# First feed-forward: seven quarter products for the second half's hidden groups, and the modulation sums laid out anew

## The chip, the cores and the metric

The kernel runs on one core of one Trainium2 chip, as one program. The metric is the device time of one execution in microseconds (us). The kernel before takes 2897.2 us, the median of three runs (2896.49 to 2897.56).

## What is computed

The reference runs 512 tokens of width 1024 through two stacks of layers. The change touches the first of them, whose layers are modulated by a condition vector `c`:

```
cond = jax.nn.silu(c)
mod = (cond @ ada_w[i] + ada_b[i]).reshape(b_, N_SUBLAYERS, 3, D_MODEL)
h = adaln(x, norm_g[i, 0], mod[:, 0, 0], mod[:, 0, 1])
x = x + 0.5 * (1.0 + mod[:, 0, 2][:, None, :]) * swiglu(h, ffn_w_in[i, 0], ffn_w_out[i, 0])
...
def swiglu(h, w_in, w_out):
    g, u = jnp.split(h @ w_in, 2, axis=-1)
    return (jax.nn.silu(g) * u) @ w_out
```

All products are in float32 accuracy. There are six modulated sublayers, numbered s = 0 to 5; 0, 2, 3 and 5 are feed-forwards of this kind with 2816 hidden columns, 1 is a pooling mixer and 4 an attention. `cond @ ada_w` asks for 6 x 24 = 144 sums of 128 outputs each. Sixteen of them (shift and scale of s = 0) are needed before the first layer can begin, the other 128 are "modulation sums" in what follows, in the order s = 0 (8 of them, the gate), then 24 for each later s.

## The kernel before, in words

Weights come from HBM as chunks of 128 x 1024 floats (512 KB) into a ring of four buffers, `raw`. Each chunk is split into a high part `wh` (ScalarE, L697) and a low part `wl` (VectorE, L1263, the "weight split"), and TensorE makes three products for each 128 x 128 block of weights: high by high, high by low, low by high. The activations are split alike: `HH` and `HL` are the normed input of a feed-forward, `AH` and `AL` the hidden activations. A ring buffer may be split again when TensorE has used its chunk, so a split is at most four chunks ahead.

A feed-forward is done in two halves. Each half has a first map (6 or 5 hidden groups of 256 hidden columns, each with four chunks: 8 input tiles, 4 output tiles, so 96 matmuls of 512 columns) and a second map (12 or 10 chunks, in two banks of four output tiles). A hidden group ends with silu on ScalarE, a product and the low part on VectorE (`hidden_group`, L1603 and L1622). The two halves of `PS` (PSUM) are used in turn: a group may begin when the group two before it has been read (`bank_free`).

In the feed-forwards s = 2, 3 and 5 most hidden groups are "fast groups" (4 of 6 and 5 of 5; the table `FAST`): the matrix product is cut in four quarters of weights and four quadrants of activations, and made by seven quarter products, not eight. A fast group has 7 x 24 = 168 matmuls of 256 columns (L2478 to L2480). It wants four mixed quadrants of the input, made once per feed-forward by VectorE and ScalarE (`whole`, `mixed_input`, `mix_low`, `mix_high`: 12 VectorE instructions), and for each group four sums of weight quarters and seven splits on VectorE (`fast_low`: L1654 is the split, L1657, L1660, L1662 and L1664 the sums). The products of a fast group follow each other as (i, 1), (i, 7), (i, 6), (i, 2), (i, 5), (i, 3), (i, 4), with (i+1, 1) ahead of (i, 3). Six buffers hold the quarters: the four of `raw` and two halves of `WK`. SyncE issues these loads in order at L581, and the first two go into `WK`.

The modulation sums are VectorE instructions over 128 x 1024 (`ada_sum`, L1333; the sum is read out by a short second instruction). Their weights, 512 KB each, are loaded by GpSimd's queue: the first 80 into a ring of three tiles (L618), all during s = 0; then 24 each in s = 2 and s = 3 (L626) into four tiles: `piece`, `HT` and the two halves of `WK`. `ADA_PHASES` says that 16 of these lie in the first half's second map and 8 in the second half's. `splits_with_sums` puts a number of sums behind each weight split.

At the start of the fast groups of a second half, VectorE makes `fast_low` for two products, adds the second map's result to `X` (`add_out`, L1328) and goes on with `fast_low` for the third:

```
for k in range(early):
    fast_low(part, k)
if between:
    between()
...
for k in range(early, RING):
    fast_low(part, k)
```

Of the kernel before, what the change touches and what calls it, by code (L numbers as in the profile page):

```python
# [20 lines left out]
ALU = mybir.AluOpType  # L21
# [38 lines left out]
ADA_RING = 3  # L60
# [71 lines left out]
def make_plan(upto=None):  # L132
# [24 lines left out]
    for i, (kind, f) in enumerate(seq):  # L157
# [12 lines left out]
        elif kind == "ffn":  # L170
            st["parts"], st["sets"] = [], sum(bool(p.get("parts")) for p in plan[:-1])
            for half, (ng, nt) in enumerate(f["halves"]):
                nf = (f.get("fast") or (0, 0))[half]
                if nf:
# [5 lines left out]
                                            tile=2 * (ng - nf), sums=ADA_BY[f["gate"]] - ADA_PHASES[1] if late else 0))  # L180
# [35 lines left out]
def build(nc, A, out, upto=None):  # L216
    plan, NCH = make_plan(upto)
    ctx = ExitStack()
    with ctx:
# [27 lines left out]
        with ExitStack() as temps:  # L247
# [36 lines left out]
        ada_late = [piece[:, 0:1024], HT[:, :, :].rearrange("p a t -> p (a t)"),  # L284
                    *(WK[:, 2 * i:2 * i + 2, :].rearrange("p k t -> p (k t)") for i in range(2))]
        ada_tiles = [acc[:, 1, 1024:2048], acc[:, 1, 2048:3072], piece[:, 0:1024]]
# [46 lines left out]
        def mix_raw(i):  # L333

            o = 2048 + 1024 * i + (2048 if i >= 4 else 0)
            return arena[:, o:o + 1024].rearrange("p (k t) -> p k t", k=4)
# [61 lines left out]
        ada_in = [sem(f"ada_in{i}") for i in range(ADA_RING)]  # L398
        ada_late_in = [sem(f"ada_late_in{i}") for i in range(4)]
# [112 lines left out]
        def _(sp):  # L512
# [34 lines left out]
            sp.dma_start(bands[:, 0:NBAND], A["params"][:, NCOL:NCOL + NBAND]).then_inc(bands_in, 16)  # L547
# [36 lines left out]
            for st in plan:  # L584
                for part in st.get("parts", ()):
# [6 lines left out]
                    loaded = part["c"] + RING  # L592
            load_chunks(loaded, NCH)
# [10 lines left out]
        def _(pl):  # L604
# [9 lines left out]
            pl.wait_ge(ada0_step, 14)  # L614
            for m, (s, j) in enumerate(ADA_ORDER[:ADA_EARLY]):
                if m >= ADA_RING:
                    pl.wait_ge(ada_step, m + 1 - ADA_RING)
                pl.dma_start(ada_tiles[m % ADA_RING], A["stream"][NCH + s * NADA + j, :, :]).then_inc(ada_in[m % ADA_RING], 16)  # L618
            m = ADA_EARLY
            for st in plan:  # L620
                for part, n in zip(st.get("parts", ()) if st.get("gate") in ADA_BY else (), ADA_PHASES):
                    pl.wait_ge(a_ready, part["e"] + part["n"] + 1)
                    for i in range(n):
                        pl.wait_ge(ada_step, max(m - 3, ADA_EARLY))
                        s, j = ADA_ORDER[m]
                        pl.dma_start(ada_late[m % 4], A["stream"][NCH + s * NADA + j, :, :]).then_inc(ada_late_in[m % 4], 16)  # L626
                        m += 1
# [57 lines left out]
        def _(act):  # L685
# [202 lines left out]
            def mix_high(i, sets):  # L888

                act.wait_ge(mix_sum, 4 * sets + i + 1)  # L890
                src = mix_raw(4 + i)
# [51 lines left out]
            for st in plan:  # L943
# [32 lines left out]
                elif kind == "ffn":  # L976
                    e, cv, j = st["e"], st["cv"], 0
                    c_last = c + sum(4 * ng + nt for ng, nt in st["halves"]) - 4 * sum(part["n"] for part in st["parts"])
                    for ng, nt in st["halves"]:
                        pairs = ng // 2  # L980
                        if st["parts"]:
                            part = st["parts"][c > st["c"]]
                            if c == st["c"]:
                                if part is fast_parts[0]:
                                    F(condc, condb, ACT.Copy).then_inc(cond_moved, 1)
                                    act.wait_ge(cond_moved, 1)
# [11 lines left out]
                        if st is plan[2] and c == st["c"]:  # L998
# [22 lines left out]
                        if st is plan[2] and c < c_last - nt:  # L1021
                            late_constants()
                        for half in range(2):
                            if half == 1 and c + nt // 2 == c_last:
                                tilewise_tail(st, c, nt)
                            else:
                                split_until(c + nt // 2 + RING)
                            c += nt // 2
# [220 lines left out]
        def _(dve):  # L1249
# [46 lines left out]
            def late_constants():  # L1296
# [5 lines left out]
                link(nc.vector.tensor_tensor_reduce(WK[:, 0, 0:64], P("lam", 0, 64), P("lam", 64, 64), 1.0, 0.0,  # L1302
                                                    ALU.mult, ALU.add, lam[:, 0:1]))
                nc.vector.tensor_tensor_reduce(WK[:, 0, 64:128], P("lam", 128, 64), P("lam", 192, 64), 1.0, 0.0,
                                               ALU.mult, ALU.add, lam[:, 1:2]).then_inc(lam_dot, 1)

                for i, (nm, f) in enumerate([("fq", 0.125), ("fk", 1.0), ("aq", 0.125), ("ak", 1.0), ("bq", 0.125),
                                             ("bk", 1.0), ("bsub", (1.0 - 0.2) * math.sqrt(128))]):
                    TS(gains[:, i:i + 1], P(nm), f, None, ALU.mult)
                dve.wait_ge(sp_exp, 1)  # L1310
# [20 lines left out]
            def ada_sum(tile, s, j, cond=condb):  # L1331

                return nc.vector.tensor_tensor_reduce(tile, tile, cond, 1.0, 0.0, ALU.mult, ALU.add, mod[:, s, j:j + 1])  # L1333
# [38 lines left out]
            def ada_until(n):  # L1372

                while at["ada"] < n:
                    m = at["ada"]
                    s, j = ADA_ORDER[m]
                    if m < ADA_EARLY:
                        dve.wait_ge(ada_in[m % ADA_RING], 16 * (m // ADA_RING + 1))
                        ada_sum(ada_tiles[m % ADA_RING], s, j).then_inc(ada_step, 1)
                    else:  # L1380
                        dve.wait_ge(ada_late_in[m % 4], 16 * ((m - ADA_EARLY) // 4 + 1))
                        ada_sum(ada_late[m % 4], s, j, condc).then_inc(ada_step, 1)
# [241 lines left out]
            def whole(k, t, i):  # L1624

                link(TT(mix_raw(i), quadrant(HH, k, t).bitcast(F32), quadrant(HL, k, t).bitcast(F32), ALU.add))

            def mixed_input(i, a, b, op):

                dve.wait_ge(vec_step, at["step"])  # L1630
                if op is None:
# [1268 lines left out]
```

## Time and profile before

| | |
|---|---|
| median of three runs | 2897.2 us |
| time of the profiled execution | 2896.0 us |
| its span, first to last instruction | 2893.6 us |
| TensorE matmuls busy | 2873.8 us (99%) |
| VectorE busy | 1939.4 us (67%) |
| ScalarE busy | 1264.7 us (44%) |
| TensorE's mean granted clock | 0.999 |

The time of an execution is 2.4 us longer than its span. Busy time of TensorE is a union of overlapping instructions, so at 99% the question is at what pace the matmuls follow each other, and where they don't.

### The profile page before, as it was taken

The page shows a single profiled execution, that of the slowest core. Times are in us where ns is not written, and L with a number is a line of the kernel's source. Part 1 is how long each engine was busy: PE and PEld are TensorE (multiplying, and loading weights), DVE is VectorE, ACT ScalarE, POOL GpSimd, SP SyncE. Part 2 cuts the span into 40 slices and gives each one's busy share as a digit, 9 for nine tenths or more (in the row PEclk, how much of TensorE's full clock was granted, in tenths as well). Part 3 has the DMA queues.
Part 4 walks back from the last instruction along what each step waited for, and adds up shares of the span by engine and source line. Part 5 has one row for each costly group of instructions (what it writes and reads, how often), then busy time and mean ns, then how long its engine had stood idle before and what let it go on. Part 6 is the DMA issues. An engine that isn't in the chain of part 4 may idle for free. (4 is left out here: it accounts for less than half of the span.)

```text
span 2893.6 us, 40922 instructions
## 1 busy us (share of the span) xinstructions
PE 2873.8 (99%) x16099; PEld 2485.7 (86%) x16099; DVE 1939.4 (67%) x2624; ACT 1264.7 (44%) x1752; POOL 144.9 (5%) x297
## 2 busy tenths in 40 slices
PE   8999999999999999999999999999999999999999
PEld 7888889899898998868999988788888888888887
DVE  8667688777786777876856758766535467754453
ACT  4223255344452445474533445654414348443332
POOL 0111100100001001040000000200000001000000
PEclk9999999999999999999999999999999999999999
DMA  7867613524236243251332322413232222232231
GB/s 299 272 217 255 210 45 115 206 109 154 89 115 230 91 168 107 88 182 61 108 126 79 114 91 88 160 63 110 87 105 98 95 81 95 96 108 95 88 109 66
DMA packets 100944, 366.99 MB, mean 127 GB/s; under 512 B 11248, under 2 KB 11808, under 8 KB 100784
## 3 DMA queue, kind: packets, MB, share of 16 engines
q1 hardware_dynamic: 77616, 276.56, 27.9%
q0 software_dynamic: 23168, 88.17, 8.8%
q8 instruction: 116, 1.90, 0.3%
q14 instruction: 44, 0.36, 0.0%
HBM read 362.51 MB, written 2.18 MB: 126 GB/s over the span
## 5 line engine op out<-in xcount | busy, mean ns | idle before, releaser
L1263 DVE TENSOR_TENSOR wl<-raw,wh 128x1024 fp32r<-128x1024 f32 x393 | 477.1, 1226 | 519.4 <-ACT wh L697 518.9
L697 ACT ACTIVATE wh<-raw 128x1024 fp32r<-128x1024 f32 x393 | 409.8, 1054 | 752.4 <-PE PS L2131 685.1
L2131 PE MATMUL PS<-HH,wh 128*128 128x512 f32 x1560 | 608.2, 390 | 0.4 <-DVE HL L1979 0.3
L2131 PE MATMUL PS<-HL,wh 128*128 128x512 f32 x1560 | 607.7, 390 | 0.0
L2131 PE MATMUL PS<-HH,wl 128*128 128x512 f32 x1560 | 607.7, 390 | 0.0
L2131 PEld LDWEIGHTS PS<-HH,wh 128*128 128x128 f32 x1560 | 293.1, 188 | 62.1 <-DVE HL L1979 0.8
L2131 PEld LDWEIGHTS PS<-HH,wl 128*128 128x128 f32 x1560 | 293.0, 188 | 60.5
L2131 PEld LDWEIGHTS PS<-HL,wh 128*128 128x128 f32 x1560 | 293.1, 188 | 60.3
L2131 PE MATMUL PS<-AH,wh 128*128 128x512 f32 x848 | 330.7, 390 | 0.5 <-DVEq L2014 0.5
L2131 PE MATMUL PS<-AL,wh 128*128 128x512 f32 x848 | 330.5, 390 | 0.0
L2131 PE MATMUL PS<-AH,wl 128*128 128x512 f32 x848 | 330.3, 390 | 0.0
L2480 PE MATMUL PS<-HH,wl 128*128 128x256 f32 x864 | 245.0, 284 | 0.0
L2479 PE MATMUL PS<-HL,wh 128*128 128x256 f32 x864 | 245.0, 284 | 0.0
L2478 PE MATMUL PS<-HH,wh 128*128 128x256 f32 x864 | 244.9, 283 | 0.0
L2131 PEld LDWEIGHTS PS<-AH,wh 128*128 128x128 f32 x848 | 159.3, 188 | 33.7 <-DVEq L2014 0.9
L2131 PEld LDWEIGHTS PS<-AH,wl 128*128 128x128 f32 x848 | 159.3, 188 | 33.0
L2131 PEld LDWEIGHTS PS<-AL,wh 128*128 128x128 f32 x848 | 159.4, 188 | 32.5
L2480 PE MATMUL PS<-TH,wl 128*128 128x256 f32 x648 | 183.8, 284 | 0.0
L2478 PE MATMUL PS<-TH,wh 128*128 128x256 f32 x648 | 183.7, 284 | 0.0
L2479 PE MATMUL PS<-TL,wh 128*128 128x256 f32 x648 | 183.7, 284 | 0.0
L1654 DVE TENSOR_TENSOR wl<-raw,wh 128x1024 fp32r<-128x1024 f32 x117 | 142.7, 1222 | 38.6 <-ACT wh L910 38.6
L2479 PEld LDWEIGHTS PS<-HL,wh 128*128 128x128 f32 x864 | 166.1, 192 | 0.5
(346 smaller groups left out, 5107.6 us busy)
## 6 DMA issues: line engine op xcount, KB each, us to landing
raw<-in_stream SPq DMA_DIRECT2D x459, 512.0 KB, 3.4
acc<-in_stream POOLq DMA_DIRECT2D x54, 512.0 KB, 4.9
WK<-in_stream SPq DMA_DIRECT2D x42, 512.0 KB, 4.5
piece<-in_stream POOLq DMA_DIRECT2D x38, 512.0 KB, 5.0
WK<-in_stream POOLq DMA_DIRECT2D x24, 512.0 KB, 6.6
arena<-in_stream SPq DMA_DIRECT2D x16, 512.0 KB, 12.5
HT<-in_stream POOLq DMA_DIRECT2D x12, 512.0 KB, 6.8
TBa<-negcum POOLq DMA_DIRECT2D x8, 640.0 KB, 5.0
```

Source lines behind the costliest of these rows:

```text
L697: F(wh[:, r, :], raw[:, r, :], ACT.Copy).then_inc(hi_done, 1)
L1263: TT(wl[:, r, :], raw[:, r, :], wh[:, r, :].bitcast(F32), ALU.subtract).then_inc(lo_done, 1)
L1654: TT(wl[:, r, :], src, wh[:, r, :].bitcast(F32), ALU.subtract).then_inc(fast_lo, 1)
L2131: mm = MM(PS[g % 2][:, j, :], l, x, start=(first and i == 0), stop=(last and i == 2), skip_group_check=after_halves)
L2478: MM(o, wh[:, r, w], xh, start=first, stop=False, skip_group_check=True)
L2479: MM(o, wh[:, r, w], xl, start=False, stop=False, skip_group_check=True)
L2480: mm = MM(o, wl[:, r, w], xh, start=False, stop=kk == 3, skip_group_check=True)
```

## The change

`FAST` gets the entry `0: (0, 5)`: the five hidden groups of the second half of the first feed-forward become fast groups. Their mixed input is made during the first half's plain groups. The modulation sums are laid out anew: 36 in the first half's plain groups of s = 0 (two behind each split, three in the last group), then 20 and 10 in its second maps; 20 and 11 in those of s = 2 and of s = 3. All of them use one list of seven tiles (`ADA_PLACES`), the last four of a first half only `piece` and `HT`. The spread condition vector lies in `bands` (`condc`) from the start, so the bands of the pooling mixer are loaded late and the vector is moved away and back. The small constants for later layers (`late_constants`) move into the first half's second map and are cut in two, with `late_factors` behind `add_out`.

```diff
-FAST = {2: (4, 5), 3: (4, 5), 5: (4, 5)}
-ADA_BY = {0: 8 + 3 * NADA, 2: 8 + 4 * NADA, 3: 8 + 5 * NADA}
-ADA_EARLY = ADA_BY[0]
-ADA_PHASES = (16, 8)
+FAST = {0: (0, 5), 2: (4, 5), 3: (4, 5), 5: (4, 5)}
+ADA_EARLY = 36
+ADA_PHASES = {0: (20, 10), 2: (20, 11), 3: (20, 11)}
+ADA_BY = {0: 66, 2: 97, 3: 128}
+ADA_PLACE = [2, 3, 0] + [4, 5, 6]
+def late_places():
+
+    places = []
+    for into_part, behind in ADA_PHASES.values():
+        places += [(0, 1, 2, 3)[i % 4] if i < into_part - 4 else i % 2 for i in range(into_part)]
+        places += [(0, 1, 2, 3)[i % 4] for i in range(behind)]
+    return places
...
-                                            tile=2 * (ng - nf), sums=ADA_BY[f["gate"]] - ADA_PHASES[1] if late else 0))
+                                            tile=2 * (ng - nf), sums=max(m + 1 for m in range(ADA_BY[f["gate"]] - ADA_PHASES[f["gate"]][1])
+                                                      if ADA_PLACES[m] in (2, 3)) if late else 0))
...
-            pl.wait_ge(ada0_step, 14)
-            for m, (s, j) in enumerate(ADA_ORDER[:ADA_EARLY]):
-                if m >= ADA_RING:
-                    pl.wait_ge(ada_step, m + 1 - ADA_RING)
-                pl.dma_start(ada_tiles[m % ADA_RING], A["stream"][NCH + s * NADA + j, :, :]).then_inc(ada_in[m % ADA_RING], 16)
+            pl.wait_ge(ht_done, KT)
+            def load_ada(m):
+
+                if ada_free(m):
+                    pl.wait_ge(ada_step, ada_free(m))
+                (s, j), place = ADA_ORDER[m], ADA_PLACES[m]
+                pl.dma_start(ada_tiles[place], A["stream"][NCH + s * NADA + j, :, :]).then_inc(ada_in[place], 16)
...
+                    if part:
+                        pl.wait_ge(a_ready, part["e"] + part["n"] + 1)
                     for i in range(n):
+                        if not part and ADA_PLACES[m] == 1:
+                            pl.wait_ge(mix_ready, 4)
+                        load_ada(m)
                         m += 1
...
+                            act.wait_ge(ada_step, ADA_EARLY)
+                            for i in range(4):
+                                mix_high(i, st["sets"])
...
+                                    ada_until(at["ada"] + (3 if u == 5 else 2))
+                                    if (u, i) == (2, 1):
+                                        whole(0, 0, 0, sets)
+                                    elif (u, i) == (2, 3):
+                                        whole(0, 1, 1, sets)
+                                    elif (u, i) == (3, 0):
+                                        mixed_input(0, sets)
...
+                            for i in range(4):
+                                mix_low(i, sets)
...
-                                splits_with_sums(c + nt // 2 + RING, 2 if st["parts"] else 1, ada or at["ada"])
-                                if half == 1 and st["parts"]:
-                                    fast_groups(st, st["parts"][1],
+                                ahead = c + nt != c_last and st["at"][1]
+                                most = 0 if ada is None else ada - ADA_PHASES[st["gate"]][1] if ahead else ada
+                                if st is plan[2] and half == 0 and ahead:
+                                    late_constants()
+                                splits_with_sums(c + nt // 2 + RING, 2, most)
+                                if half == 1 or not ahead:
+                                    ada_until(most)
+                                if half == 1 and ahead:
+                                    fast_groups(st, ahead,
                                                 lambda: add_out(st, g, c + nt // 2, 4, gate))
                                 else:
                                     add_out(st, g, c + nt // 2, 4 * half, gate)
+                                if st is plan[2] and half == 0 and ahead:
+                                    late_factors()
```

VectorE in s = 0, where the first half's second map ends and the second half's first map begins (`piece` and `acc` are the tiles of weights for sums, `X` the residual). Before:

```order
L1263 TENSOR_TENSOR wl<-raw,wh 128x1024
L1333 ISA piece,mod<-piece,acc 128x1024
L1333 ISA mod 128x1
L1263 TENSOR_TENSOR wl<-raw,wh 128x1024
L1333 ISA acc,mod<-acc 128x1024
L1333 ISA mod 128x1
L1263 TENSOR_TENSOR wl<-raw,wh 128x1024
L1333 ISA acc,mod<-acc 128x1024
L1333 ISA mod 128x1
L1328 SCALAR_TENSOR_TENSOR X<-PS,mod,X 128x512 x4
```

The same place in the changed kernel, from the second sum in `WK` behind the last split (L1701 and L1704 are `fast_low`'s split and first sum of quarters):

```order
L1381 ISA WK,mod<-WK,bands 128x1024
L1381 ISA mod 128x1
L1381 ISA piece,mod<-piece,bands 128x1024
L1381 ISA mod 128x1
L1381 ISA HT,mod<-HT,bands 128x1024
L1381 ISA mod 128x1
L1381 ISA piece,mod<-piece,bands 128x1024
L1381 ISA mod 128x1
L1381 ISA HT,mod<-HT,bands 128x1024
L1381 ISA mod 128x1
L1546 TENSOR_TENSOR mod<-mod,par 128x24
L1548 SCALAR_TENSOR_TENSOR mod<-mod,par 128x8
```

One more instruction on `mod` follows and then L1701. Four sums with no split between them now stand ahead of the first quarter split, where each sum stood behind a split before.

VectorE at the end of the first half's last plain group in s = 0 (L1603 and L1622 are `hidden_group`). Before:

```order
L1263 TENSOR_TENSOR wl<-raw,wh 128x1024
L1333 ISA acc,mod<-acc 128x1024
L1333 ISA mod 128x1
L1603 TENSOR_TENSOR PR<-SG,PS 128x1024
L1622 TENSOR_TENSOR AL<-PR,AH 128x1024
```

And in the changed kernel, where L1647 and L1666 are `hidden_group`, and L1688 and L1690 the low parts of the mixed input:

```order
L1308 TENSOR_TENSOR wl<-raw,wh 128x1024
L1381 ISA acc,mod<-acc,bands 128x1024
L1381 ISA mod 128x1
L1381 ISA acc,mod<-acc,bands 128x1024
L1381 ISA mod 128x1
L1381 ISA acc,mod<-acc,bands 128x1024
L1381 ISA mod 128x1
L1647 TENSOR_TENSOR PR<-SG,PS 128x1024
L1666 TENSOR_TENSOR AL<-PR,AH 128x1024
L1688 TENSOR_TENSOR TL<-acc,TH 128x1024 x3
L1690 TENSOR_TENSOR HL<-HT,HH 128x4x256
```

Two more sums stand behind the last split, and four low parts behind the group.

## Rows read from the trace of the kernel before

**Rows 1.** The page: busy time, share of the span, instructions

```profile
PE 2873.8 (99%) x16099; PEld 2485.7 (86%) x16099; DVE 1939.4 (67%) x2624; ACT 1264.7 (44%) x1752; POOL 144.9 (5%) x297
```

**Rows 2.** Waits of TensorE: line, who released it; us in total, times, longest

```profile
PE PS L2492 <- DMA ident<-in_ident: 3.3, 1, 3.3
PE PS L2247 <- ACT HH L761: 2.2, 1, 2.2
...
PE PS L2131 <- DVE HL L1979: 0.3, 1, 0.3
```

**Rows 3.** Timeline of TensorE, s = 0: start us, us; second maps and plain groups begin

```profile
149.06 0.39 PE L2131 MATMUL PS<-AH,wh 128*128 128x512 f32 x1
...
214.34 0.39 PE L2131 MATMUL PS<-HH,wh 128*128 128x512 f32 x1
...
323.14 0.39 PE L2131 MATMUL PS<-AH,wh 128*128 128x512 f32 x1
```

**Rows 4.** Timeline of TensorE, s = 2: its fast groups begin and end

```profile
454.76 0.28 PE L2478 MATMUL PS<-HH,wh 128*128 128x256 f32 x1
...
538.14 0.40 PE L2131 MATMUL PS<-AH,wh 128*128 128x512 f32 x1
...
600.72 0.28 PE L2478 MATMUL PS<-HH,wh 128*128 128x256 f32 x1
```

**Rows 5.** Windows, s = 0's last plain groups: us, busy of PE, PEld, DVE, ACT, POOL, clock, DMA, GB/s

```profile
128.00:150.00 22.00, 22.00 (x99) 18.23 (x98) 15.18 (x20) 6.34 (x7) 3.70 (x7) 1.00 0.79 260
```

**Rows 6.** Timeline of VectorE, s = 0: a last plain group's end, then the late constants

```profile
150.41 1.23 DVE L1263 TENSOR_TENSOR wl<-raw,wh 128x1024 fp32r<-128x1024 f32 x1 [1.92 <-ACT wh L697]
151.56 1.22 DVE L1333 CUSTOM_DVE_ANT_0 acc<-acc 128x1024 f32<-128x1024 f32 x1
152.70 1.22 DVE L1603 TENSOR_TENSOR PR<-SG,PS 128x1024 f32<-128x1024 f32 x1
155.04 1.23 DVE L1622 TENSOR_TENSOR AL<-PR,AH 128x1024 fp32r<-128x1024 f32 x1 [1.12 <-ACT AH L886]
...
157.33 0.17 DVE L1299 TENSOR_SCALAR sp<-par 128x8 f32<-128x8 f32 x1
...
158.66 0.16 DVE L1284 TENSOR_SCALAR sp<-sp 128x8 f32<-128x8 f32 x1
...
162.10 1.22 DVE L1263 TENSOR_TENSOR wl<-raw,wh 128x1024 fp32r<-128x1024 f32 x1
```

**Rows 7.** Timeline of VectorE, s = 2: from the sixteenth sum to the fast groups

```profile
582.60 1.22 DVE L1333 CUSTOM_DVE_ANT_0 WK<-WK,bands 128x1024 f32<-128x1024 f32 x1
583.75 0.08 DVE L1333 DVE_READ_ACCUMULATOR2_ANT mod<- 128x1 f32 x1
591.20 1.23 DVE L1654 TENSOR_TENSOR wl<-WK,wh 128x1024 fp32r<-128x1024 f32 x1 [7.37 <-ACT wh L910]
592.34 1.22 DVE L1657 TENSOR_TENSOR WK<-WK 128x1024 f32<-128x1024 f32 x1
596.63 1.23 DVE L1654 TENSOR_TENSOR wl<-WK,wh 128x1024 fp32r<-128x1024 f32 x1 [3.08 <-ACT wh L910]
597.78 1.22 DVE L1660 TENSOR_TENSOR WK<-WK,raw 128x1024 f32<-128x1024 f32 x1
599.03 1.22 DVE L1662 TENSOR_TENSOR WK<-WK 128x1024 f32<-128x1024 f32 x1
600.92 2.73 DVE L1328 SCALAR_TENSOR_TENSOR X<-PS,mod,X 128x512 f32<-128x512 f32 x4 [0.67 <-PE PS L2131]
603.57 1.22 DVE L1654 TENSOR_TENSOR wl<-WK,wh 128x1024 fp32r<-128x1024 f32 x1
```

**Rows 8.** Instructions on the tile HT, 530 to 610 us: its loads

```profile
DMA to landing us min/median/max: 3.8/6.0/7.6
```

**Rows 9.** Timeline of SyncE's queue, s = 2: the first six loads of quarters

```profile
583.91 0.81 SPq L581 DMA_DIRECT2D WK<-in_stream  x2
584.78 2.06 SPq L581 DMA_DIRECT2D raw<-in_stream  x4
```

**Rows 10.** DMA in 575 to 605 us: rate in 40 slices, then KB and us to landing

```profile
GB/s 306 300 169 38 5 0 0 0 11 0 0 0 0 153 306 415 431 410 410 421 426 426 421 355 22 0 0 0 0 0 0 0 0 0 0 0 22 0 0 0
...
raw<-in_stream SPq DMA_DIRECT2D x4, 512.0 KB, 6.6
```

**Rows 11.** Windows around the pooling mixer, columns as in group 5

```profile
400.00:404.00 4.00, 2.69 (x19) 2.12 (x17) 4.00 (x11) 2.30 (x5) 0.00 (x0) 1.00 0.09 37
404.00:408.00 4.00, 3.29 (x18) 3.26 (x18) 3.12 (x12) 1.41 (x4) 0.00 (x0) 0.67 0.00 0
408.00:412.00 4.00, 3.19 (x22) 2.92 (x22) 3.42 (x9) 2.28 (x6) 0.00 (x0) 0.90 0.00 0
```

More of the change, by code:

```diff
@@ L170, in make_plan @@
         elif kind == "ffn":
-            st["parts"], st["sets"] = [], sum(bool(p.get("parts")) for p in plan[:-1])
+            st["parts"], st["at"], st["sets"] = [], [None, None], sum(bool(p.get("parts")) for p in plan[:-1])
             for half, (ng, nt) in enumerate(f["halves"]):
@@ L592, in _ @@
                     loaded = part["c"] + RING
+                if st is plan[2]:
+                    load_chunks(loaded, part["c"] + st["halves"][1][1] + 1)
+                    loaded = part["c"] + st["halves"][1][1] + 1
+                    sp.wait_ge(cond_moved, 1)
+                    sp.dma_start(bands[:, 0:NBAND], A["params"][:, NCOL:NCOL + NBAND]).then_inc(bands_in, 16)
             load_chunks(loaded, NCH)
@@ L1775, in _ @@
                     ada = ADA_BY.get(st["gate"])
[L1776 to L1777 removed]
+                    sets = st["sets"]
+                    for part, (ng, nt) in zip(st["at"], st["halves"]):
+                        if part:
                             if c == st["c"]:
[L1779 removed]
+                                dve.wait_ge(cond_moved, 2)
                                 dve.wait_ge(h_ready, st["h"])
[L1781 to L1783 removed]
+                                whole(0, 0, 0, sets)
+                                whole(0, 1, 1, sets)
+                                mixed_input(0, sets)
@@ L1801, in _ @@
-                        if ada and not st["parts"]:
-                            paired = st is plan[2] and c == st["c"]
-                            if paired:
-                                split_until(c + 10)
-                                hidden_group(st, e, g, cv, j, 0, 0)
-                                split_until(c + 11)
-                                hidden_group(st, e + 1, g + 1, cv + 1, j + 1, 2, 0)
-                                split_until(c + 12)
-                                e, cv, g, c, j = e + 2, cv + 2, g + 2, c + 8, j + 2
-                            for u in range(2 if paired else 0, ng):
+                                fast_groups(st, part, None)
@@ new lines, in _ @@
+                            e, cv, g, c, j, ng = e + ng, cv + ng, g + ng, part["c"], j + ng, 0
+                        elif st is plan[2]:
+                            split_until(c + 10)
+                            hidden_group(st, e, g, cv, j, 0, 0)
+                            split_until(c + 11)
+                            hidden_group(st, e + 1, g + 1, cv + 1, j + 1, 2, 0)
+                            split_until(c + 12)
+                            e, cv, g, c, j = e + 2, cv + 2, g + 2, c + 8, j + 2
+                            for u in range(2, ng):
@@ L1828, in _ @@
                         e, cv, g, c, j = e + 2 * pairs, cv + 2 * pairs, g + 2 * pairs, c + 8 * pairs, j + 2 * pairs
-                        if ng % 2 and not ada and not st["parts"]:
+                        if ng % 2 and not part:
                             split_until(c + 4 + RING)
@@ L2520, in _ @@
                                 group(c, g, KT, h_tile, h_ready_at, nm=nm)
-                                if not st["parts"] or st["parts"][0]["c"] > c + 4:
+                                if not st["at"][0] or st["at"][0]["c"] > c + 4:
                                     group(c + 4, g + 1, KT, h_tile)
                             c, g, e2, pairs, nm = c + 8, g + 2, e2 + 2, pairs - 1, None
-                        if st["parts"]:
-                            part = st["parts"][half]
+                        part = st["at"][half]
+                        if part:
                             fast_groups(st, part)
@@ L2541, in _ @@
                                 group(c, g, nt, a_tile, (lambda k: [(a_ready, e + k // 2 + 2)]),
-                                      begun=1 if half == 0 and st["parts"] else 0)
+                                      begun=1 if half == 0 and part else 0)
                             c, g = c + nt // 2, g + 1
```

136 lines of the change are left out of this document (72 added, 64 removed).

## The prediction, as it was made before the changed kernel ran

> **What bounds the kernel now.** I read the page first: TensorE's matmuls cover 99% of the span, VectorE 67% [rows 1]. Then the waits of TensorE: apart from the start, where it waits for inputs, no line waits more than some 2 us in total, and no fast-group line stands in the list at all [rows 2]. So TensorE's instruction stream sets the time, and an edit is worth what it takes out of that stream, less the waits that it makes. The timeline gives the pace. In s = 0 the second half's five plain groups run from 214.34 to 323.14 us [rows 3]: 480 matmuls in 108.80 us, 0.2267 us each, 21.76 us a group. In s = 2 four fast groups, with one unit of 12 plain matmuls put among them, run from 454.76 to 538.14 us [rows 4]: 83.38 us, less 12 x 0.2267 = 2.72, leaves 80.66, so 20.16 us a group and 0.120 us a matmul, exactly even. There was no wait in them.
>
> **What the change takes out.** Five groups, each 21.76 - 20.16 = 1.60 us: **8.0 us**. The bytes are the same (20 quarters for 20 chunks), and the unit of 12 is only moved. [...]
>
> **What it adds to VectorE, first half of s = 0.** One VectorE instruction over 128 x 1024 behind another costs 1.14 us: the split starts at 150.41, the sum at 151.56, the product at 152.70 [rows 6]. A plain group of 21.76 us now holds 4 splits, 8 sums, 2 instructions of the group and 2 or 3 of the mixed input: 16 or 17 instructions, 18.2 to 19.4 us, and with the 1.12 us for ScalarE's copy [rows 6] 19.4 to 20.5. The last has 12 sums and none of the input: 18 instructions, 21.6 us. Before it was 15.18 us of 22 [rows 5]. That just fits. A split is four chunks (21.8 us) ahead, less some 2.6 for both engines' parts, so VectorE may be some 14 us late before TensorE misses one. I put this at nothing. The loads go from 7 + 4 to at most 8 + 4 of 512 KB per group, 289 GB/s by their bytes where 260 at 0.79 of the DMA engines is the row [rows 5] and 431 the highest rate seen [rows 10]: also nothing.
>
> **Where it is late: the second map of the first half.** It begins at 149.06 us [rows 3] in both kernels. The last split of the plain group starts at 150.4 as now [rows 6]. Behind it: three sums until 155.0, product, ScalarE's copy and low part until 158.5, four low parts of the mixed input until 162.8 (ScalarE's highs, some 1.05 each, keep pace), first part of the late constants 1.3 us (157.33 to 158.66 [rows 6]), a split and a sum: 166.5. The second sum reads `HT`, whose load GpSimd may issue only after the fourth low part, at 162.8; such a load took 3.8 to 7.6 us, median 6.0 [rows 8]. So about 168.5. From there VectorE has 15 sums and 7 splits (22 x 1.14 = 25.1 us), `add_out` 2.7 us [rows 7] and `late_factors`, 158.66 to 162.10, 3.4 us [rows 6]: 199.7, say 200. In s = 2 the same sixteenth sum ends at 583.75 us [rows 7], 16.97 us before its fast groups; here it is 214.34 - 200 = 14.3 us before. Where four tiles can't be refilled in time, up to 2 us later still.
>
> **The four sums that stand alone.** The thirteenth sum ends 4.6 us before the sixteenth, so the reloaded `piece` is there 1.5 us after it (6.0 median), and the seventeenth and eighteenth sum end at 203.6. The twentieth reads `HT` again: load 6.0 us, sum 1.2 us: 210.9. Then the chain that s = 2 shows [rows 7]: three small instructions on `mod` (0.6), split 1.1, sum 1.25, ScalarE 1.15, split 1.3, two sums 2.4, `add_out` 2.65, the third split 1.2: 11.7 us, ends **222.6**. TensorE wants that third product at 214.34 + 2 x 24 x 0.120 = **220.1**. The wait is **2.5 us**. Behind it one split more is ready each time TensorE asks, and the wait is not given back, since TensorE has no slack. Bounds: `HT` in 3.8 us and the eighteenth sum at 202.0 give 218.8, no wait; 7.6 us and everything 2 us later give 226.3, a wait of 6.2.
>
> During these loads SyncE issues six quarters from the sixteenth sum on: in s = 2 at 583.91 to 586.8 [rows 9], and the engines run full at 410 to 431 GB/s for 7 us, so that a quarter in `raw` lands after 6.6 us [rows 10]. No row has a load of GpSimd's beside them; this is why I don't go below the median. The Trainium skill ("DMA: Bandwidth & Descriptors", section "Queues, rings and completion order") says that each DMA engine takes turns between the queues that have work, packet by packet. By that the load would not stand behind all six; in order behind them it would land some 9 us after its issue, 3 us more wait.
>
> **In s = 2 and s = 3** the same four sums and three more in the second half come in. VectorE is idle for 7.37 us there [rows 7]. Seventeenth and eighteenth end at 586.0, the twentieth at 586.1 + 6.0 + 1.2 = 593.3, the third split at 593.3 + 11.1 = 604.4, wanted at 600.72 + 5.76 = 606.5: no wait; with 7.6 us 606.0, still none. I count 0.1 us each, bound 1. Their second halves have 27 us for 11 sums; add_out is then some 4 us later and its next user waits for nothing in the rows. Nothing. The bands of the pooling mixer are loaded some 40 us ahead of their use: nothing.
>
> **Sum.** 8.0 - 2.5 - 0.2 = 5.3 us. The profiled execution took 2896.0 us and would take 2890.7; the median of the runs is 1.2 us above it, so **2891.9 us**.
>
> **Rivals.** (1) *All is hidden.* For it: fast groups show no wait anywhere [rows 2], and the least landing gives 218.8. Against it: nothing in s = 2 has the late constants, `add_out` and the input's low parts in the same stretch. Gain 6.8 to 8.0 us, 2889.2 to 2890.4. (2) *Larger waits.* `HT` lands after the six quarters, or the clock falls. TensorE was busy for 2.69 of 4 us around 402 us, and the granted clock was then 0.67 and 0.90 for 4 us each [rows 11]: between its levels of 1.2 and 2.4 GHz that is about 3.4 us at the lower, 1.7 us lost. With a wait of 4.5 to 6.2 us and this, the gain is 0 to 3.5 us: 2893.7 to 2897.2. (3) *Slower.* VectorE becomes the bound in the plain groups: if mixed input and sums there cost 3.5 us a group more than the ledger (because loads from GpSimd's queue come late, say), it ends the fourth group 14 us late, misses splits from then on, and all of it stands again ahead of the fast groups, since VectorE never comes to rest between. At 5 us a group it is 20 us late; less the 14 us of lead, 6 us of waits in the plain groups and 6 more ahead of the fast ones against 8 gained: 2901. It decides from about 4 us a group. Against it: 6.8 us of 22 are idle now [rows 5]. (4) *A quarter product is no faster in this place*: the pace is TensorE's own; I see nothing for it.
>
> **How the numbers follow.** A measurement of this kernel can tell about 0.2%, 5.8 us, from no change. My forecast (wait 1.2 to 4.5 us, gain 3.5 to 6.8) 0.47; all hidden 0.25; larger waits 0.20; slower 0.08. The forecast straddles the 5.8 us: 0.18 of its 0.47 lie above. Faster 0.25 + 0.18 = 0.43; slower by over 5.8 us 0.05; within 0.52. The range, 2888.8 to 2895.6, takes in the hidden case and half of the larger waits.
>
> **What would show it.** The first of s = 0's fast groups begins at 214.3 and its five take 5 x 20.16 us plus the wait; TensorE's waits list a fast-group line released by VectorE's quarter split, about 2.5 us, once, near 220 us, and none in s = 2 and 3. `late_factors` stands behind `add_out` near 190 us, the sixteenth sum near 200, the twentieth near 211. The plain groups keep their 21.76 us. I am wrong if there is no such wait, if it sits at the first product or in s = 2, or if TensorE waits before 214 us.

## The result, and the profile after

The changed kernel takes 2902.6 us (median of 8 runs, 2900.5 to 2908.1), the kernel before beside it 2896.6. The ratio is 1.0022, 95% interval 1.0013 to 1.0031. A second measurement gave 2899.5 us (11 runs, 2897.6 to 2903.3) against 2896.5, 1.0011 (1.0002 to 1.0020). So the change costs some 3 to 6 us; forecast were 5.3 gained. The profiled execution took 2901.7 us, its span is 2899.8. Two executions further down, 3527.4 us with four tiles and 3131.6 us with the late factors moved, ran at a mean granted clock of 0.75 and 0.85 and are left out of the ratios (the median of 2897.0 us given for the latter kernel is 2896.6 without it).

The page of the changed kernel, as [rows 1] of before:

```profile
PE 2870.9 (99%) x16459; PEld 2499.7 (86%) x16459; DVE 1998.3 (69%) x2681; ACT 1288.6 (44%) x1784; POOL 145.2 (5%) x297
```

TensorE is busy for 2.9 us less, and the span is 6.2 us longer: time was lost in waits. They are in the timeline of TensorE (start us, us, and in brackets the idle time ahead of the instruction and who ended it), at the head of the fast groups of s = 0, where the first three rows are the first, second and third quarter product, and at the third one of s = 2 and s = 3:

```profile
217.51 0.35 PE L2546 MATMUL PS<-HH,wh 128*128 128x256 f32 x1 [2.52 <-DVE wl L1701]
221.00 0.35 PE L2546 MATMUL PS<-TH,wh 128*128 128x256 f32 x1 [0.38 <-DVE wl L1701]
227.16 0.55 PE L2546 MATMUL PS<-TH,wh 128*128 128x256 f32 x1 [3.07 <-DVE wl L1701]
...
327.53 0.40 PE L2199 MATMUL PS<-AH,wh 128*128 128x512 f32 x1
...
609.84 0.36 PE L2546 MATMUL PS<-TH,wh 128*128 128x256 f32 x1 [0.99 <-DVE wl L1701]
...
958.92 0.36 PE L2546 MATMUL PS<-TH,wh 128*128 128x256 f32 x1 [1.11 <-DVE wl L1701]
```

The last plain matmul ahead of them starts at 214.61. At the plain pace of 0.22 us TensorE wanted the first product at 214.83, and 48 matmuls of 0.120 us later, at 220.6, the third; it began at 227.16, 6.6 us late. 6.0 of that are the waits as the profile counts them. The rest is overlap that is lost at each: a wait is counted from the end of the matmul before, and without it the next one would have started some 0.16 us ahead of that end. The same stretch on VectorE's timeline, to be held against [rows 7]; `L1381` are sums, `L1701` splits:

```profile
200.27 1.22 DVE L1381 CUSTOM_DVE_ANT_0 WK<-WK,bands 128x1024 f32<-128x1024 f32 x1
201.42 0.08 DVE L1381 DVE_READ_ACCUMULATOR2_ANT mod<- 128x1 f32 x1
201.42 1.22 DVE L1381 CUSTOM_DVE_ANT_0 piece<-piece,bands 128x1024 f32<-128x1024 f32 x1
203.35 1.23 DVE L1381 CUSTOM_DVE_ANT_0 HT<-HT,bands 128x1024 f32<-128x1024 f32 x1 [0.71 <-DMA HT<-in_stream]
211.10 1.23 DVE L1381 CUSTOM_DVE_ANT_0 piece<-piece,bands 128x1024 f32<-128x1024 f32 x1 [6.51 <-DMA piece<-in_stream]
214.25 1.23 DVE L1381 CUSTOM_DVE_ANT_0 HT<-HT,bands 128x1024 f32<-128x1024 f32 x1 [1.92 <-DMA HT<-in_stream]
...
216.14 1.23 DVE L1701 TENSOR_TENSOR wl<-WK,wh 128x1024 fp32r<-128x1024 f32 x1
217.28 1.22 DVE L1704 TENSOR_TENSOR WK<-WK 128x1024 f32<-128x1024 f32 x1
219.63 1.23 DVE L1701 TENSOR_TENSOR wl<-WK,wh 128x1024 fp32r<-128x1024 f32 x1 [1.13 <-ACT wh L950]
...
223.16 2.72 DVE L1376 SCALAR_TENSOR_TENSOR X<-PS,mod,X 128x512 f32<-128x512 f32 x4
225.80 1.22 DVE L1701 TENSOR_TENSOR wl<-WK,wh 128x1024 fp32r<-128x1024 f32 x1
```

The sixteenth sum ends at 201.4, and the seventeenth to twentieth stand alone behind it. VectorE is idle for 6.51 and 1.92 us ahead of the last two, and each of those ends when its load lands. GpSimd's queue issued them here:

```profile
202.94 0.53 POOL L654 DMA_DIRECT2D piece<-in_stream  x1 [3.78 <-DVE mod L1381]
205.14 0.53 POOL L654 DMA_DIRECT2D HT<-in_stream  x1 [1.67 <-DVE mod L1381]
```

and SyncE's queue issued the six quarters here, as in [rows 9]:

```profile
201.59 0.99 SPq L609 DMA_DIRECT2D WK<-in_stream  x2
202.63 2.42 SPq L609 DMA_DIRECT2D raw<-in_stream  x4
```

The view of the DMA from 203 to 216 us (KB each, us from issue to landing), beside [rows 10], where such a quarter in `raw` took 6.6 us:

```profile
raw<-in_stream SPq DMA_DIRECT2D x4, 512.0 KB, 10.5
piece<-in_stream POOLq DMA_DIRECT2D x1, 512.0 KB, 8.1
HT<-in_stream POOLq DMA_DIRECT2D x1, 512.0 KB, 9.1
```

[Rows 8] had 7.6 us as the longest landing in `HT`. The same view in short windows tells where the time goes. From 203.5 to 206.5 us SyncE's queue moves 0.97 MB and GpSimd's nothing, though the load into `piece` was issued at 202.94. From 207 to 212 us both move the same, 1.01 MB and 0.98 MB. So this load stood still for some 4 us and then had half of the rate, and the load into `HT`, 2.2 us behind it in the same queue, with it. At last the windows behind the waits (us, then busy time of PE, PEld, DVE, ACT, POOL, granted clock, DMA share, GB/s):

```profile
224.00:226.00 2.00, 0.10 (x1) 0.00 (x0) 2.00 (x4) 2.00 (x4) 0.00 (x0) 1.00 0.00 0
226.00:228.00 2.00, 0.83 (x4) 0.87 (x5) 2.00 (x2) 0.43 (x1) 0.00 (x0) 0.52 0.00 0
228.00:230.00 2.00, 2.00 (x11) 2.00 (x11) 2.00 (x3) 0.00 (x0) 0.00 (x0) 0.50 0.00 0
230.00:232.00 2.00, 2.00 (x12) 2.00 (x10) 2.00 (x3) 0.00 (x0) 0.00 (x0) 0.50 0.15 39
232.00:234.00 2.00, 2.00 (x15) 2.00 (x15) 0.69 (x1) 1.34 (x2) 0.00 (x0) 0.77 1.00 377
```

Behind the third wait TensorE runs at the lower of its two levels, 1.2 GHz, for some 6 us: 11 to 12 matmuls in 2 us where 19 is the pace. From the third product to the second map 100.37 us pass; in the kernel with more tiles, below, which keeps the full clock there, it is 97.78. So the lower clock cost a further 2.6 us.

### The profile page after: what moved, and what is told of

Its sections match the earlier page's. It is cut to its first block and busy times, and to the rows that moved or that the text cites. A ratio compares the mean times of both kernels' runs of the same rounds, so it can differ in the third digit from the quotient of the medians.

```text
span 2899.8 us, 41648 instructions
## 1 busy us (share of the span) xinstructions
PE 2870.9 (99%) x16459; PEld 2499.7 (86%) x16459; DVE 1998.3 (69%) x2681; ACT 1288.6 (44%) x1784; POOL 145.2 (5%) x297
## 5 line engine op out<-in xcount | busy, mean ns | idle before, releaser
L2199 PE MATMUL PS<-HH,wh 128*128 128x512 f32 x1400 | 545.1, 389 | 0.4 <-DVE HL L2047 0.4
L2199 PE MATMUL PS<-HL,wh 128*128 128x512 f32 x1400 | 544.7, 389 | 0.0
L2199 PE MATMUL PS<-HH,wl 128*128 128x512 f32 x1400 | 544.6, 389 | 0.0
L2199 PEld LDWEIGHTS PS<-HH,wh 128*128 128x128 f32 x1400 | 262.8, 188 | 56.0 <-DVE HL L2047 0.8
L2199 PEld LDWEIGHTS PS<-HH,wl 128*128 128x128 f32 x1400 | 262.8, 188 | 54.7
L2546 PE MATMUL PS<-HH,wh 128*128 128x256 f32 x1024 | 289.9, 283 | 2.5 <-DVE wl L1701 2.5
L2547 PE MATMUL PS<-HL,wh 128*128 128x256 f32 x1024 | 289.9, 283 | 0.0
L2548 PE MATMUL PS<-HH,wl 128*128 128x256 f32 x1024 | 289.8, 283 | 0.0
L2546 PE MATMUL PS<-TH,wh 128*128 128x256 f32 x768 | 218.7, 285 | 5.5 <-DVE wl L1701 5.5
L2547 PE MATMUL PS<-TL,wh 128*128 128x256 f32 x768 | 218.4, 284 | 0.0
L2546 PEld LDWEIGHTS PS<-HH,wh 128*128 128x128 f32 x1024 | 196.7, 192 | 3.4 <-issue 2.9
L1701 DVE TENSOR_TENSOR wl<-raw,wh 128x1024 fp32r<-128x1024 f32 x138 | 168.3, 1221 | 43.9 <-ACT wh L950 43.9
L2548 PEld LDWEIGHTS PS<-HH,wl 128*128 128x128 f32 x1024 | 196.7, 192 | 0.0
```

Source lines behind the costliest of these rows:

```text
L1701: TT(wl[:, r, :], src, wh[:, r, :].bitcast(F32), ALU.subtract).then_inc(fast_lo, 1)
L2199: mm = MM(PS[g % 2][:, j, :], l, x, start=(first and i == 0), stop=(last and i == 2), skip_group_check=after_halves)
L2546: MM(o, wh[:, r, w], xh, start=first, stop=False, skip_group_check=True)
L2547: MM(o, wh[:, r, w], xl, start=False, stop=False, skip_group_check=True)
L2548: mm = MM(o, wl[:, r, w], xh, start=False, stop=kk == 3, skip_group_check=True)
```

## The experiments

Three theories stood against each other. **L**, late loads: the 19th and the 20th sum use `piece` and `HT` again, so their loads can't be issued before the 17th and 18th sum end, and then lie beside six quarters. **W**, work: VectorE's own instructions (late constants, mixed input, sums) make the quarter splits late by themselves. **C**, clock: the lower clock behind the wait is a price of its own. Each edit is to the changed kernel; ratios are to the kernel before on the same chip.

**Four tiles for the last four sums** (places 7 and 8 of the list of tiles are now `SG` and `PR`).

```
-places += [(0, 1, 2, 3)[i % 4] if i < into_part - 4 else i % 2 for i in range(into_part)]
+places += [(0, 1, 2, 3)[i % 4] if i < into_part - 4 else (0, 1, 7, 8)[i % 4] for i in range(into_part)]
...
+  *(tile[:, :, :].rearrange("p a t -> p (a t)") for tile in (SG, PR))]
```

> The last four sums of a first half's second map read four tiles in turn (piece, HT, and two tiles that are idle there, SG and PR), so that the loads for the 19th and 20th sum need not wait for the 17th and 18th and can be issued before SyncE's six quarters. Theory L (late loads: the waits of 2.52 and 3.07 us at the fast groups' head come from the loads of the 19th and 20th sum, 8.1 and 9.1 us to landing): the 20th sum ends near 207 us and not 215.4, the third quarter split near 219, before TensorE asks at 220.6; the s = 0 waits (6.0 us) and the 3.2 us of the lower clock behind them go, and most of the 2.1 us of waits in s = 2 and s = 3: 2889 to 2893 us. Theory W (VectorE's own work: late constants, mixed input, sums and add_out make the split late by themselves): more than 2 us of waits remain in s = 0, 2898 to 2903.

2889.9 us, ratio 0.9976 (0.9966 to 0.9985): faster than either kernel. In this run's timeline of GpSimd's queue all four loads are issued before 200 us:

```profile
196.86 0.53 POOL L655 DMA_DIRECT2D piece<-in_stream  x1 [7.85 <-DVE mod L1382]
198.26 0.53 POOL L655 DMA_DIRECT2D HT<-in_stream  x1 [0.88 <-DVE mod L1382]
198.78 0.53 POOL L655 DMA_DIRECT2D SG<-in_stream  x1
199.50 0.53 POOL L655 DMA_DIRECT2D PR<-in_stream  x1 [0.18 <-issue]
```

and on VectorE the twentieth sum and the third split follow so:

```profile
206.79 1.23 DVE L1382 CUSTOM_DVE_ANT_0 PR<-PR,bands 128x1024 f32<-128x1024 f32 x1 [0.69 <-DMA PR<-in_stream]
...
218.35 1.22 DVE L1702 TENSOR_TENSOR wl<-WK,wh 128x1024 fp32r<-128x1024 f32 x1
```

The third split ends at 219.6, wanted at 220.7, and no quarter product waits in s = 0, 2 or 3. VectorE does all the work that theory W blames, with the same instructions in the same order. So L stands, and W as the whole cause falls. TensorE's timeline gives the gross gain at the same time; its rows are the first and the third fast product and the second map:

```profile
214.91 0.28 PE L2547 MATMUL PS<-HH,wh 128*128 128x256 f32 x1
...
220.66 0.28 PE L2547 MATMUL PS<-TH,wh 128*128 128x256 f32 x1
...
318.44 0.40 PE L2200 MATMUL PS<-AH,wh 128*128 128x512 f32 x1
```

103.53 us, less 12 x 0.2267 = 2.72 for the unit of plain matmuls in between, is 100.81 for five groups, 20.16 each. The 8.0 us are real.

**The same again,** on another chip:

> The kernel with four tiles for the last four sums, on another day of the same comparison: 6.6 us below the kernel before, as in its first run (2889.9 against 2896.5), within 1.5 us, no wait at any quarter product, third split of s = 0 about 1 us before it is wanted. If the first result was the luck of one chip, as the changed kernel's 2902.6 and 2899.5 show that a chip or a call can differ by 3 us: 2890 to 2893 and a wait in s = 0.

2889.4 us, 0.9975 (0.9966 to 0.9984), and the profile again lists no wait at a quarter product. But I had expected the third split some 1 us early, and it ends at 220.70 with 220.74 wanted; its product starts 0.1 us late. The gain of some 7 us holds, with a margin of 1.1 us at this place in one trace and of nothing in the other.

**Sixteen sums ahead, the rest behind.**

```
-ADA_PHASES = {0: (20, 10), 2: (20, 11), 3: (20, 11)}
+ADA_PHASES = {0: (16, 14), 2: (16, 15), 3: (16, 15)}
...
-places += [(0, 1, 2, 3)[i % 4] if i < into_part - 4 else i % 2 for i in range(into_part)]
+places += [(0, 1, 2, 3)[i % 4] if i < into_part - 4 or into_part == 16 else i % 2 for i in range(into_part)]
```

The change of the places belongs to it: with no sums alone ahead of the fast groups, the last four of the sixteen again take turns over all four tiles, the two halves of `WK` too.

> Sixteen sums in the first halves' second maps in place of twenty, and four more behind, in the second halves' (14, 15, 15 in place of 10, 11, 11): no sums stand alone ahead of the fast groups. Theory L: as with more tiles, the waits at the head of the fast groups go in s = 0, 2 and 3; VectorE is nearly 5 us of work lighter there than with more tiles, so none can be left. 2889 to 2893, plus at most 1 us for each of the three second maps if the sums behind them now end late. Theory W, in its form that blames late constants, mixed input and add_out and not the lone sums: at least 2 us of wait stay at the third quarter split of s = 0, 2896 or more.

2904.2 us, ratio 1.0028 (1.0017 to 1.0039): both theories missed. The waits at the fast groups are gone, as L says, but others take their place at the end of the second halves' second maps. In this kernel's waits of TensorE:

```profile
PE PS L2413 <- DVE X L1576: 10.0, 3, 4.1
```

They stand at 365.04 [1.79], 749.34 [4.09] and 1103.50 us [4.11], one for each second half. VectorE shows why at the second: the fifteenth sum ends at 738.2, and only then come `add_out`, two weight splits and the additions into `X` (L1576) that the last matmuls wait for.

```profile
730.76 1.23 DVE L1381 CUSTOM_DVE_ANT_0 WK<-WK,bands 128x1024 f32<-128x1024 f32 x1 [1.99 <-DMA WK<-in_stream]
...
737.05 1.23 DVE L1381 CUSTOM_DVE_ANT_0 WK<-WK,bands 128x1024 f32<-128x1024 f32 x1
738.21 2.72 DVE L1376 SCALAR_TENSOR_TENSOR X<-PS,mod,X 128x512 f32<-128x512 f32 x4
740.85 1.22 DVE L1308 TENSOR_TENSOR wl<-raw,wh 128x1024 fp32r<-128x1024 f32 x1
```

I had allowed 1 us for each. Ten and eleven sums fit behind (there is no such wait in the changed kernel); fourteen cost 1.8 us, fifteen 4.1 us each.

**The same in s = 0 alone.**

```
-ADA_PHASES = {0: (20, 10), 2: (20, 11), 3: (20, 11)}
+ADA_PHASES = {0: (16, 14), 2: (20, 11), 3: (20, 11)}
```

The line of places is changed as in the run before.

> The same in s = 0 alone; s = 2 and s = 3 keep 20 and 11. Theory L: 9.2 us less than the changed kernel (6.0 of waits and 3.2 of clock), near 2893.4; what remains against the run with sixteen everywhere is the 2.1 us of waits in s = 2 and 3, each at the third quarter product. If s = 2 and 3 cost as much as s = 0 through something not seen as a wait, it is over 4 us above that run.

2896.2 us, 0.9999 (0.9990 to 1.0008). The waits of s = 0's head are away, one of 2.20 us at 365.56 is new, and the third quarter products of s = 2 and s = 3 wait 1.34 and 1.10 us. That is 2.8 us above the 2893.4 that I expected, and the wait of 2.20 us is most of it. It lies 8 us under the run with sixteen everywhere, not above it, since the tails of s = 2 and 3 wait 8.2 us there and their heads 2.4 here.

**Idle products in the wait.**

```
+if part is fast_parts[0] and k == 2:
+    for _ in range(12):
+        MM(PS[g % 2][:, 3, :], identb[:, :], identb[:, :].unsqueeze(1).broadcast_to((128, 4, 128)),
+           start=True, stop=True, skip_group_check=True)
```

> The changed kernel with 12 idle products (128x128 by 128x512, their result is read by nobody) on TensorE ahead of the third quarter product of s = 0's fast groups, 2.6 us, which fill the wait of 2.52 us. Theory C (the lower clock from 226 to 233 us follows TensorE's pause and costs 3.2 us beside the wait itself): the granted clock stays at 1.00 there, or falls only for the second wait at 227.2; 1 to 3 us less than the changed kernel, 2899.5 to 2901.5. Against it: the clock falls all the same (the second wait of 3.07 us is enough), or the added products only add: 2902 to 2905.

2900.6 us, 1.0013 (1.0004 to 1.0022). In its profiled execution the clock was lower behind the first wait, which has no such products ahead of it:

```profile
218.00:220.00 2.00, 2.00 (x13) 2.00 (x12) 0.88 (x2) 1.06 (x1) 0.00 (x0) 0.59 0.00 0
220.00:222.00 2.00, 2.00 (x12) 2.00 (x11) 1.97 (x3) 0.19 (x1) 0.00 (x0) 0.56 0.00 0
```

The lower clock there cost nothing of its own: the third split ended only at 226.8, TensorE filled with idle products until then, and from its third product at 227.05 to the second map it took 97.95 us, as at full clock. The median is within the expected range, but it can't tell: two things moved at once. So both waits were filled:

**Idle products in all long waits** (11 ahead of the first, 15 ahead of the third product of s = 0, 5 ahead of the third in s = 2 and s = 3).

> The changed kernel with idle products ahead of every long wait of its fast groups: 11 ahead of the first quarter product of s = 0 (2.4 us), 15 ahead of the third (3.3 us), 5 (1.1 us) ahead of the third of s = 2's and s = 3's. VectorE is as late as before, TensorE only does not stand still meanwhile. If the lower clock is the price of the pause (theory C), the granted clock is 1.00 from 214 to 236 us and about 3.2 us come back, and the runs lie closer together than the changed kernel's 2900.5 to 2908.1: median 2899 to 2900. If the clock falls by itself, or the added products cost what they save: 2902 to 2904.

2900.9 us, 1.0015 (1.0006 to 1.0024). The granted clock is 1.00 in every 2 us from 214 to 236, and the runs lie within 3.0 us (5.7 for the changed kernel beside it). But the median is 1.4 us above the changed kernel's, not 3 below. Some 0.5 us of that the products cost themselves: the third split ends near 225.9, the fifteen end with 226.8, and the third product starts at 226.47. So the lower clock is real in the profiled executions, with a price that the traces agree on: from the third product to the second map it is 100.4 to 100.6 us in the three traces that have it there (the changed kernel's two and the one with the late factors moved), and 97.8 to 98.0 in the eight that don't, this one among them. It also goes with the slower executions (mean granted clock 0.999 in the fastest of the changed kernel's eleven runs, 0.997 in the slowest). But the medians speak against 3 us of it in a typical execution, and C as I held it falls; with intervals of 2.6 us either way they don't say more.

**The changed kernel once more.**

> The changed kernel once more, beside the others on one chip: 2902.5 us, waits of some 6 us at the head of s = 0's fast groups and some 2 us in s = 2 and s = 3, and a stretch of some 3 to 7 us at a granted clock near 0.5 behind the waits of s = 0. If the lower clock is a matter of chance from one execution to the next, this one may show it elsewhere or for another length; the start's windows from 16 to 24 us then also show 1.00 or less with no edit between.

2899.5 us, 1.0011 (1.0002 to 1.0020), 3 us under what I expected: this is the second measurement given with the result. Its profiled execution (2903.3 us, the slowest of its runs) waits 1.70, 0.38 and 3.06 us in s = 0, 2.65 in s = 2, 1.05 in s = 3, and shows 0.50 from 226 to 232 us, and 0.57 and 0.58 in the 4 us behind the wait in s = 2. The start's windows show 0.67 and 0.90.

**Late factors moved.**

```
-if st is plan[2] and half == 0 and ahead:
+if st is plan[2] and half == 0 and not ahead:
     late_factors()
```

> The changed kernel with late_factors (3.4 us of small VectorE instructions) moved from the first half's second map of s = 0 to the second half's, so that all sums from there on can be 3.4 us earlier. If VectorE's backlog passes on into the late loads (the 17th and 18th sum end earlier, so their successors' loads are issued earlier): the 20th sum ends near 212 us and not 215.4, the first wait of s = 0 (2.52) goes, the third split ends at 223.6 against 220.6 wanted, so about 3.0 of 6.0 us of wait are left: 2898 to 2900 us. If the loads ahead of the 17th and 18th sum set the pace anyway: no change, 2901 to 2903. That it cures all of it (theory W, VectorE's work alone): 2891 to 2893.

2897.0 us, 1.0002 (0.9992 to 1.0011). The first wait is gone, the third is 2.74 us (with some 7 us of the lower clock behind it), the twentieth sum ends at 212.1. The trace did what the first case says; the median is 1 us better than it. It shows that VectorE's backlog counts, but as a delay of the loads: with 3.4 us less work ahead, 3 of 6 us of wait are left, and the two loads take as long as before, 8.6 and 9.3 us. In s = 2 and s = 3 waits of 1.60 and 0.96 us stay.

**Quarter loads held back.**

```
-sp.wait_ge(ada_step, part["sums"])
+sp.wait_ge(ada_step, part["sums"] + 2)
```

> The changed kernel with SyncE's six quarter loads held back until two sums later (the 18th and not the 16th has ended, some 3.5 us). Theory L in the form that blames the transfers beside it: the 19th sum's load, issued near 203 us, lands alone in 3.4 to 4 us and not 8.1; the 20th's, issued at the moment at which the quarters are, lands in 4 to 5 us if it goes ahead of them (then the 20th sum ends near 210.5, the third split near 222.1, some 1.5 us of wait in s = 0 are left, no lower clock: 2894 to 2896 us), and in 8 to 9 if it takes turns with them (then 20th sum and waits as in the changed kernel, 2901 to 2903). The quarters themselves land some 3.5 us later, which the first two products do not feel.

2896.0 us, 0.9998 (0.9989 to 1.0007). In this kernel's instructions on `piece` from 195 to 216 us:

```profile
DMA to landing us min/median/max: 3.6/3.6/3.6
```

The 19th sum's load takes 3.6 us where it took 8.1, with the same bytes and issued at 202.54 where it was 202.94: the 4.5 us were the quarters beside it. The 20th's, issued at 204.60, half a us behind the first quarters, takes 6.9: neither ahead of them (4 to 5) nor as late as in turns at full length (8 to 9). The third wait is 3.05 us, with no lower clock behind it. No wait in s = 2 and s = 3.

**Both together.**

> late_factors moved and the quarter loads held back by two sums, both in one kernel. If the two parts of the delay add (VectorE's backlog of 3.4 us, and the 19th and 20th load beside six quarters, 3 to 4 us), the 20th sum of s = 0 ends near 209 us, the third split near 220.7, just when it is wanted: no wait or under 0.5 us in s = 0, no lower clock, 2889.5 to 2892. If one of them only uncovers the other (the load for the 20th sum still takes 6.9 us behind the 18th), 1 to 3 us of wait remain: 2893 to 2896.

2891.2 us, 0.9982 (0.9973 to 0.9991). The time is that of the first case, the trace that of the second: the 20th's load, issued at 201.99, takes 7.9 us to its use at 209.94, and one wait is left, 2.24 us ahead of the third product, none in s = 2 and s = 3. The two repairs together are worth what more tiles are worth, less 1.5 us.

**The kernel before, profiled again.**

> The kernel before, profiled once more. Two terms that the change doesn't touch stand against it in every trace of the changed kernels: a start up to 0.9 us later (the second map of s = 0 begins at 148.7 to 150.0 us, 149.06 before), and 4.7 to 5.1 us from the last matmul to the end of the span, 3.65 before. If they are chance, they may show here too: 149.5 and 4.7 to 5.1. If they belong to the change: 149.0 and 3.7 again.

The start is chance: the second map begins at 149.63 us, 0.57 later than [rows 3], with 0.79 and 0.78 as the clock from 16 to 24 us and no edit between. The end is not: 3.71 us from the last matmul, as before. The eleven traces of the changed kernel and its variants have 4.7 to 5.1. The view of the DMA over the last 12 us shows a difference: each of the eleven has a row that neither trace of before has. The changed kernel's:

```profile
q14 instruction: 1, 0.01, 0.2%
```

and its instructions on `out` there have a longest landing of 3.2 us:

```profile
DMA to landing us min/median/max: 2.0/2.6/3.2
```

Before it is 2.1; over the eleven it is 3.0 to 3.2. The profile calls this queue's packets instructions. In the changed kernel the one packet lies between 2894 and 2896 us, while the last rows are written. That it is the cause of the longer landing was not tried, nor which part of the change brought it there.

## Why the prediction was wrong, point by point

- **Gross gain 8.0 us: right.** 100.81 us for five groups where 108.80 stood.
- **The plain groups keep 21.76 us: right.** No wait stands before 214 us; VectorE is busy for 19.1 to 20.6 us of 22 in the last three groups, near the 18.2 to 20.5 us of instructions that the sum had. The lead of 14 us beside it is short of a term: four chunks less 2.6 us are 19.2, and 14 comes out only if the chunk in use, 5.4 us, is taken off too; no run tests it. Rival 3 (VectorE the bound there) did not happen, and the kernel still came out slower.
- **Place and releaser: right in part.** The wait is at s = 0's fast groups and is ended by the quarter split, and the third product is its longest. But it begins at the first product already (2.52 us), which the sum did not have, and another sits in s = 2 (0.99 us): two of the signs that the prediction named for being wrong.
- **The step that failed is the landing of the two last loads, "load 6.0 us".** It was 8.1 and 9.1, and the delay of the third product 6.6 us, not 2.5. I took the median of [rows 8] because no row had such a load beside six quarters; [rows 10] showed the same engines full for 7 us, and that should have moved the value to or over the upper bound, not left it in the middle. The sentence on "in order behind them", 3 us more wait, was nearer (the load did take 9.1); holding the quarters back showed 3.6. The rule of the Trainium skill ("DMA: Bandwidth & Descriptors", section "Queues, rings and completion order"), turns between the queues packet by packet, agrees with the trace where both queues move data: 256 packets of GpSimd's queue and 277 of SyncE's from 207 to 212 us. Turns alone don't give the 9.1: GpSimd's queue moved nothing from 203.5 to 206.5 us, and when the load into `HT` was issued, at 205.14, the one into `piece` in the same queue had still to move.
- **The sixteenth sum near 200: 1.4 us late** (0.5 of it the start), and the eighteenth 0.9. With 0.5 us from the end of a sum to the issue of the next load, which the sum had at nothing, and 3.1 us from the load this makes the twentieth 4.5 us late, 215.4 for 210.9, and the third split 4.4, 227.0 for 222.6. The chain behind it, 11.7 us, is right to 0.1.
- **The clock stood only in a rival.** A wait of 6 us in three pieces gave 2.6 us more in the profiled execution. Rival 2 had both, with 1.7 us for the clock, and stopped at 2897.2; with the next two points it comes to some 2901.
- **s = 2 and s = 3 at 0.1 us each: too low.** 1.0 and 1.1 us, up to 2.65. The prediction put the load for the twentieth sum there at 6.0 us from issue as well; it took 8.9, and more tiles or later quarters take all of it.
- **The end of the program, 1.0 to 1.5 us, was not in the sum,** and 0.5 us each for start and pooling mixer are chance of the clock: from 380 to 424 us the mean granted clock is 0.92 in the first trace of the changed kernel and 0.96 in its second.

Against the span of 2893.6 us before: 8.0 gained; 6.6 of delay and 2.6 of clock lost at the fast groups of s = 0, 2.5 at those of s = 2 and s = 3 (2.1 of waits and the overlap lost at them), 0.5 at the start, 0.5 at the pooling mixer (the fast groups of s = 2 begin 2.2 us later than in [rows 4], the second map of s = 0, its unit of 12 counted, 1.7), 1.5 at the end. That makes 6.2 us longer, and 6.2 is measured. What stays open is how much the clock costs in a typical execution, why GpSimd's queue moves nothing for some 4 us behind an issue beside the quarters (1.0 to 1.5 us where its load is alone), and what lengthens the end.

## What to carry to other kernels

When a change puts loads in front of work with a fixed hour, write down the hour at which each can be issued, and what else the queues carry then: a tile that is refilled only when its last user is done is a chain, and its length is set by the busiest moment, not by the median. Work that is moved out of one tight place needs a slot elsewhere with its own row: sixteen sums ahead cured the head of the fast groups and lost 10 us of waits at three tails. A change can be good with a wrong list of buffers: two idle tiles made of 3 to 6 us lost 7 us gained.

## What the runs showed of the hardware

- A pause of 2 to 4 us on TensorE is followed by the lower clock in some executions and not in others. It followed waits of 2.36, 2.50, 2.65, 2.74, 3.06, 3.07 and both of 4.1 us, but not waits of 2.20, 2.24, 2.52 and 3.05 us. The Trainium skill ("TensorE: Matmul & The Clock Gate", section "What's actually happening") says that the monitor behind the clock doesn't start anew with the kernel. The runs fit that in so far as waits of one length came out both ways (2.50 and 2.52, 3.05 and 3.06 us); the spread of the times doesn't bear on it clearly: 2.1 and 2.6 us with more tiles, which have no such waits, 3.8 to 7.7 with most others, but 2.9 with sixteen sums everywhere, which has the longest.
- 512 KB from GpSimd's queue landed after 3.6 us alone, and after 6.9 to 9.3 beside six loads of SyncE's; four of those took 9.7 to 10.8 us in the median instead of 6.6. While both queues moved data they had equal shares, but GpSimd's first packets came 3.5 to 4.5 us behind the issue where SyncE had begun to issue its six loads before it, and 1.0 to 1.5 us behind it where it hadn't.
- One packet of the queue that the profile calls instruction, in the last microseconds, stands beside a longest landing of the output of 3.0 to 3.2 us in eleven traces of eleven; in the two of the kernel before there is no such packet, and it is 2.1.
